# Gate and up weights of a Strassen-style SwiGLU: two transfers of 512 KB a set in place of four of 256 KB, and operand buffers with the contraction step outside

## The reference

```python
def encoder_layer(x, ...):
    xn = rms_norm(x, norm1)
    proj = xn @ w_in
    ...                               # Hyena long convolution and windowed attention
    mixed = jnp.concatenate([rms_norm(y_hy, hy_gain), rms_norm(y_at, at_gain)], axis=-1)
    h = x + mixed @ w_out
    gu = rms_norm(h, norm2) @ w_gate_up          # (rows, 1024) @ (1024, 5632)
    gate, up = jnp.split(gu, 2, axis=-1)
    return h + (jax.nn.silu(gate) * up) @ w_down # (rows, 2816) @ (2816, 1024)
```

## Time and profile before

| | |
|---|---|
| median of 3 runs | 3033.96 us (3030.08 to 3036.27) |
| profiled execution, its own time | 3034.69 us |
| profiled execution, span of its instructions | 3032.9 us |
| mean granted TensorE clock | 0.966 of 2.4 GHz |
| TensorE busy with matmuls | 2808.7 us, 93% |
| VectorE, ScalarE, GpSimd busy | 1922.9, 1216.9, 1030.5 us |
| DMA packets in all | 362367, of them under 2 KB 301374 |
| weight transfers of gate and up | 132 and 132, of 256 KB |

### The profile page before, as it was taken

The page is one execution under the profiler, slowest core; times in us unless marked ns, Lnnn a source line. Parts: engine busy times, 40 slices in busy tenths (PEclk is TensorE's granted clock), DMA queues, the critical chain, the costliest instruction groups (busy, mean ns, idle before and its releaser), DMA issues. The chain is left out here.

```text
span 3032.9 us, 38468 instructions
## 1 busy us (share of the span) xinstructions
PE 2808.7 (93%) x14512; PEld 2546.7 (84%) x14512; DVE 1922.9 (63%) x2615; ACT 1216.9 (40%) x1939; POOL 1030.5 (34%) x797
## 2 busy tenths in 40 slices
PE   5988999899897899997799999889999988999998
PEld 4777898788786788885799999879999987999998
DVE  6765676678565666665565665756566575656655
ACT  4443554444444766664322322322232232223221
POOL 4412111122210344345533433443343344334332
PEclk9998999999998999998899999999999999999999
DMA  5475976766695435334322222332222233222221
GB/s 158 136 225 155 262 216 212 239 195 189 188 255 149 117 112 139 110 101 139 104 73 70 67 73 70 108 125 74 69 67 73 70 112 121 78 69 63 77 70 63
DMA packets 362367, 378.56 MB, mean 125 GB/s; under 512 B 43966, under 2 KB 301374, under 8 KB 361895
## 3 DMA queue, kind: packets, MB, share of 16 engines
q1 hardware_dynamic: 330312, 295.75, 33.8%
q0 software_dynamic: 31872, 80.36, 8.1%
HBM read 281.13 MB, written 94.91 MB: 124 GB/s over the span
## 5 line engine op out<-in xcount | busy, mean ns | idle before, releaser
L2502 POOL TENSOR_TENSOR ff_alo_raw<-ff_alo_raw,ff_silu 128x384 f32<-128x384 f32 x132 | 197.1, 1493 | 741.4 <-DVE ff_alo_raw L2703 658.0
L2725 DVE TENSOR_TENSOR ff_h<-ff_h,ff_down 128x512 f32<-128x512 f32 x396 | 265.4, 685 | 157.7 <-PE ff_down L87 157.5
L85 PE MATMUL ff_banks<-ff_xhi,ff_ghi 128*128 128x384 f32 x924 | 317.5, 344 | 34.1 <-DVE ff_glo L2713 23.5
L85 PE MATMUL ff_down<-ff_dhi,ff_ahi 128*128 128x512 f32 x792 | 312.2, 394 | 24.4 <-DVE ff_dlo L2717 16.9
L87 PE MATMUL ff_banks<-ff_xhi,ff_glo 128*128 128x384 f32 x924 | 315.3, 341 | 0.0
L86 PE MATMUL ff_banks<-ff_xlo,ff_ghi 128*128 128x384 f32 x924 | 314.3, 340 | 0.0
L85 PE MATMUL pr_acc<-pr_xhi,pr_whi 128*128 128x386 f32 (+1 forms) x864 | 306.2, 354 | 7.4 <-DVE pr_xlo L1396 7.4
L85 PE MATMUL ff_banks<-ff_xhi,ff_uhi 128*128 128x384 f32 x924 | 310.6, 336 | 2.6 <-DVE ff_ulo L2713 2.6
L86 PE MATMUL ff_down<-ff_dlo,ff_ahi 128*128 128x512 f32 x792 | 311.8, 394 | 0.0
L87 PE MATMUL ff_down<-ff_dhi,ff_alo 128*128 128x512 f32 x792 | 311.6, 393 | 0.0
L86 PE MATMUL ff_banks<-ff_xlo,ff_uhi 128*128 128x384 f32 x924 | 311.0, 337 | 0.0
(11 more groups left out here) (294 smaller groups left out, 6656.5 us busy)
## 6 DMA issues: line engine op xcount, KB each, us to landing
ff_glo_raw<-w_gate_up SPq DMA_DIRECT2D x132, 256.0 KB, 2.9
ff_ulo_raw<-w_gate_up SPq DMA_DIRECT2D x132, 256.0 KB
ff_dlo_raw<-w_down SPq DMA_DIRECT2D x66, 512.0 KB, 4.5
pr_raw<-w_in SPq DMA_DIRECT2D x108, 256.0 KB, 5.6
pr_xs<-x SPq DMA_DIRECT2D x36, 512.0 KB, 4.5
f_dram<-fi_out POOLq DMA_DIRECT2D x32, 512.0 KB, 4.1
fs_a<-f_dram SPq DMA_DIRECT2D x32, 512.0 KB, 6.7
am_q<-q_dram SPq DMA_DIRECT2D x36, 256.0 KB, 4.4
```

Source lines behind the costliest of these rows:

```text
L85: pe.matmul(out, still[0], moving[0], start=start, stop=False)
L2502: pool.tensor_tensor(block(prod, c), block(prod, c), silu[c][:], ALU.mult).then_inc(tempered, 1)
L2725: dve.tensor_tensor(h[j][:, o], h[j][:, o], down(v), ALU.add).then_inc(added, 1)
```

## The change

The dimensions of the weight buffers change places: from 7 blocks x 4 contraction steps x 128 columns to 4 contraction steps x 7 blocks x 128 columns. The blocks are renumbered so that the two column halves of one contraction half are neighbours: A12 and A22 are blocks 0 and 1, A11 and the fourth block are 2 and 3. A transfer then brings both columns' blocks of one contraction half: 128 partitions x 4 steps x 256 columns, runs of 1 KB in memory where they were 512 B. The first of the two waits for step 4 of the set before last, the second for step 5; before, the four waited for steps 0, 3, 4 and 5. In the load ahead of the stage, A12 came after two transfers of rows and now comes with the other weights. Sums, casts and subtractions read and write four runs a partition instead of one. The two parts of the split are now blocks 0 and 1 (1024 elements) and blocks 2 to 6 (2560 elements), and as A11 is in the second, TensorE waits for both parts ahead of step 0.

```diff
-    A11, A12, A22, S3, S1, S2, S4 = range(7)
+    A12, A22, A11, S3, S1, S2, S4 = range(7)
...
-    whi = [at("ghi", [P, 7, 4, P], 186560, F32R), at("uhi", [P, 7, 4, P], SB0, F32R)]
-    wlo, wraw = zip(pair("glo", [P, 7, 4, P], 186560 + 14336), pair("ulo", [P, 7, 4, P], SB0 + 14336))
+    whi = [at("ghi", [P, 4, 7, P], 186560, F32R), at("uhi", [P, 4, 7, P], SB0, F32R)]
+    wlo, wraw = zip(pair("glo", [P, 4, 7, P], 186560 + 14336), pair("ulo", [P, 4, 7, P], SB0 + 14336))
...
-        def bring_w(s, w):
+        def bring_w(s, half):
             q, p = s // 2, s % 2
             c = q % NC
             if s >= 2:
-                sp.wait_ge(multiplied, step_done(s - 2, W_STEP[w]))
+                sp.wait_ge(multiplied, step_done(s - 2, W_STEP[(S3, A22)[half]]))
             else:
                 at_least(sp, mixed, 4 * NTT * p)
-            i, half = {A11: (0, 0), A12: (0, 1), S3: (1, 0), A22: (1, 1)}[w]
-            col = FF * p + (2 * c + i) * P
-            sp.dma_start(wraw[p][:, w], w_gate_up[:, 4 * half:4 * half + 4, col:col + P]).then_inc(w_in[p], 16)
+            col = FF * p + 2 * c * P
+            sp.dma_start(wraw[p][:, :, 2 - 2 * half:4 - 2 * half].rearrange("p k i c -> p k (i c)"),
+                         w_gate_up[:, 4 * half:4 * half + 4, col:col + 2 * P]).then_inc(w_in[p], 16)
...
         def ahead():
             sp.wait_ge(handed_on, 1)
             sp.wait_ge(weighted, all_weighted)
-            for w in (A11, S3, A22):
-                bring_w(0, w)
+            for half in range(2):
+                bring_w(0, half)
             for x in (B11, T3):
                 bring_x(0, x)
-            bring_w(0, A12)
             for x in (B22, B21):
                 bring_x(0, x)
...
-                    for w in (A11, A12, S3, A22):
-                        bring_w(2 * q + 2, w)
+                    for half in range(2):
+                        bring_w(2 * q + 2, half)
...
-                for w, x in ((A11, B11), (A12, B21), (S3, T3), (A22, None)):
-                    if turning and x is not None:
-                        bring_x(g + 1, x)
-                    if q + 1 < NQ:
-                        bring_w(2 * q + 3, w)
+                if turning:
+                    bring_x(g + 1, B11)
+                    bring_x(g + 1, B21)
+                if q + 1 < NQ:
+                    bring_w(2 * q + 3, 0)
+                if turning:
+                    bring_x(g + 1, T3)
+                if q + 1 < NQ:
+                    bring_w(2 * q + 3, 1)
...
-            pool.wait_ge(w_in[p], 64 * (q + 1))
+            pool.wait_ge(w_in[p], 32 * (q + 1))
...
-            pool.tensor_tensor(raw[:, S1], raw[:, S3], raw[:, A22], ALU.add).then_inc(w_summed, 1)
+            pool.tensor_tensor(raw[:, :, S1], raw[:, :, S3], raw[:, :, A22], ALU.add).then_inc(w_summed, 1)
...
                 if at == 0:
-                    pe.wait_ge(w_low, 2 * s + 1)
-                if at == 1:
                     pe.wait_ge(w_low, 2 * s + 2)
...
-                    last = triple(pe, bank(b), (whi[p][:, w, k, :], wlo[p][:, w, k, :]), (xhi[x][:, k, :], xlo[x][:, k, :]), k == 0, k == 3)
+                    last = triple(pe, bank(b), (whi[p][:, k, w, :], wlo[p][:, k, w, :]), (xhi[x][:, k, :], xlo[x][:, k, :]), k == 0, k == 3)
...
-                act.copy(whi[p][:, 0:3], wraw[p][:, 0:3]).then_inc(w_high, 1)
+                act.copy(whi[p][:, :, 0:2], wraw[p][:, :, 0:2]).then_inc(w_high, 1)
             else:
                 act.wait_ge(w_summed, 4 * s + 4)
-                act.copy(whi[p][:, 3:7], wraw[p][:, 3:7]).then_inc(w_high, 1)
+                act.copy(whi[p][:, :, 2:7], wraw[p][:, :, 2:7]).then_inc(w_high, 1)
...
-            p, o = s % 2, slice(0, 3) if part == 0 else slice(3, 7)
+            p, o = s % 2, slice(0, 2) if part == 0 else slice(2, 7)
             dve.wait_ge(w_high, 2 * s + 1 + part)
             dve.wait_ge(w_summed, 4 * s + 4)
-            dve.tensor_tensor(wlo[p][:, o], wraw[p][:, o], whi[p][:, o].bitcast(F32), ALU.subtract).then_inc(w_low, 1)
+            dve.tensor_tensor(wlo[p][:, :, o], wraw[p][:, :, o], whi[p][:, :, o].bitcast(F32), ALU.subtract).then_inc(w_low, 1)
```

More of the change, by code:

```diff
@@ L2425, in main @@
         def main(close):
-            for w in (A11, S3, A22, A12):
-                bring_w(1, w)
+            for half in range(2):
+                bring_w(1, half)
             close()
@@ L2471, in sums @@
             raw = wraw[p]
-            pool.wait_ge(w_in[p], 64 * (q + 1))
+            pool.wait_ge(w_in[p], 32 * (q + 1))
             if s >= 2:
                 pool.wait_ge(multiplied, step_done(s - 2, 6))
-            pool.tensor_tensor(raw[:, S1], raw[:, S3], raw[:, A22], ALU.add).then_inc(w_summed, 1)
+            pool.tensor_tensor(raw[:, :, S1], raw[:, :, S3], raw[:, :, A22], ALU.add).then_inc(w_summed, 1)
             pool.wait_ge(w_summed, 4 * s + 1)
-            pool.tensor_tensor(raw[:, S2], raw[:, S1], raw[:, A11], ALU.subtract).then_inc(w_summed, 1)
+            pool.tensor_tensor(raw[:, :, S2], raw[:, :, S1], raw[:, :, A11], ALU.subtract).then_inc(w_summed, 1)
             pool.wait_ge(w_summed, 4 * s + 2)
-            pool.tensor_tensor(raw[:, S3], raw[:, A11], raw[:, S3], ALU.subtract).then_inc(w_summed, 1)
+            pool.tensor_tensor(raw[:, :, S3], raw[:, :, A11], raw[:, :, S3], ALU.subtract).then_inc(w_summed, 1)
             pool.wait_ge(w_summed, 4 * s + 3)
-            pool.tensor_tensor(raw[:, S4], raw[:, A12], raw[:, S2], ALU.subtract).then_inc(w_summed, 1)
+            pool.tensor_tensor(raw[:, :, S4], raw[:, :, A12], raw[:, :, S2], ALU.subtract).then_inc(w_summed, 1)
             pool.wait_ge(w_summed, 4 * s + 4)
@@ L2607, in weight_high @@
             if part == 0:
-                act.wait_ge(w_in[p], 64 * (q + 1))
+                act.wait_ge(w_in[p], 32 * (q + 1))
                 if s >= 2:
                     act.wait_ge(multiplied, step_done(s - 2, 5))
-                act.copy(whi[p][:, 0:3], wraw[p][:, 0:3]).then_inc(w_high, 1)
+                act.copy(whi[p][:, :, 0:2], wraw[p][:, :, 0:2]).then_inc(w_high, 1)
             else:
                 act.wait_ge(w_summed, 4 * s + 4)
-                act.copy(whi[p][:, 3:7], wraw[p][:, 3:7]).then_inc(w_high, 1)
+                act.copy(whi[p][:, :, 2:7], wraw[p][:, :, 2:7]).then_inc(w_high, 1)
         def down_high(q, i):
```

## The result

| | before | after |
|---|---|---|
| median | 3033.59 us (4 runs, 3030.08 to 3036.27) | 3052.18 us (4 runs, 3046.37 to 3055.0) |
| profiled execution, its span | 3034.69, 3032.9 us | 3046.37, 3044.6 us |
| mean granted clock | 0.966 | 0.967 |

After/before is 1.0059, with an interval of 1.0041 to 1.0078: about 18 us slower. I had forecast +7.8, and up to 3051. The profiled execution of after is its fastest run, so the spans differ by only 11.7.

The account below looks back on a forecast made before the run. TensorE was taken to bound the kernel, busy throughout steady iterations, so only its few existing waits could move: -4.4 at the start and +12.2 at the merged waits gave +7.8, 3041.8 us against the median (+0.26%), range 3033.5 to 3051.

Parts of the forecast that it names:

- 4, "At nothing": Steady iterations: fewer SyncE issues, later block requests and the new wait at steady up sets cost nothing, with 2 us of cover.
- 1 us for 1 us in 30 iterations: Steady up sets: if the 2 us of cover were gone, 30 iterations would pay 1 us each for 1 us.
- Step 3: Iteration 0 and two turns: step 0 waits for the larger part, slow clock after; 4.5, 3.1 and 4.6, together +12.2 us.
- the 2.34 for the last turn: Clock loss after the single wait at the last turn, taken as 2.34 us more because the loss there was 0 before.
- Step 1: Start of the stage: the weight set lands sooner, so GpSimd's sums and `am_xs` come sooner; -4.4 us, bounds -3 and -7.5.
- Step 2: Strided operands: four runs cost VectorE, ScalarE and GpSimd nothing; for GpSimd at most 0.5 us for three more runs.
- the start gave no 7.5: Rival: the start gains its bound of -7.5, so +4.7 in all, 3038.7 us; chance 0.13.
- the clock did not stay up: Rival: TensorE keeps full clock after the single wait, so +0.8 in all, 3034.8 us, not slower; chance 0.12.
- GpSimd paid nothing for runs: Rival: GpSimd pays 0.5 us for each sum, at the start, iteration 0 and turns; +8 on top, 3049.8 us; chance 0.12.
- the transfers did gain: Rival claimed transfers gain nothing, 512 B runs being as fast as 1 KB: +9.5 in all, 3043.5 us; chance 0.08.
- The rule weighed: Skill's 512 B minimum for line rate: longer runs would gain nothing, sum +9.5 instead of +7.8; the forecast went against it.

Follow-up runs that it names:

- e5: The changed kernel with VectorE's second part of the next gate set made one place earlier in steady iterations: 3037.41 us, ratio 1.0018 to the kernel before.
- e2: The kernel before with one edit, TensorE waits for both parts ahead of step 0: 3051.05 us, ratio 1.0057.
- e3: The kernel before with parts of 2 and 5 blocks and one wait for both, old transfers and flat layout: 3055.96 us, ratio 1.0077.
- e1: The changed kernel with the old split (three and four blocks) and the old two waits: 3028.61 us, ratio 0.9979 to the kernel before.
- e4: The kernel before with the fourth weight transfer, A12, ahead of the row transfers at the start: 3029.65 us, ratio 0.9983.
- e6: e1 with four transfers of 256 KB and runs of 512 B again, new layout kept: 3030.75 us, ratio 0.9993 to the kernel before.
- e7: e1 with both parts of the next gate set made ahead of product and down rests in each group's first chunk: 3004.22 us, ratio 0.991 to before.
- e8: The changed kernel with the moves of both e5 and e7: 3014.51 us, ratio 0.9941 to the kernel before.
- e9: e7 with second gate part and down-weight rests made earlier on VectorE in each group's last chunk: 3004.36 us, ratio 0.9896 to the kernel before.
- e10: e4 with e7's VectorE order, so old transfers, flat layout and old split: 3010.84 us, ratio 0.992 to the kernel before.

## Why the prediction was wrong

**The step that failed is 4, "At nothing".** It costed the steady iterations at nothing, after the opening had said of TensorE's existing waits that "the change can only move the time at these places". For the new wait it looked at the up sets alone: 2 us of cover, which is right. The gate sets have none. In the trace of before their second part ended 0.17 us after TensorE had begun step 0, and my own sentence there, 1 us for 1 us in 30 iterations, was the price. It came to 0.42 us in each of 27, 11.4 us in all, where 0 stood. e5 takes these gaps out of the change (about 12 us, with the `ff_dlo` wait) and e2 puts them into the kernel before (9.3 us). All of the earlier trace rows was true as well, and proved nothing: a TensorE that is busy for 100 us tells that no wait ends late, not how close one is.

**Step 3, the mechanism right and the term too large:** 9.0 us for 12.2. The merged waits came, 10.16, 10.37 and 11.32 us long, where "10 to 12" stood, and the clock behind them was 0.62, 0.63 and 0.66 (forecast 0.61). Most of the difference is the position: I let step 0 start where step 1 had, plus 0.2 at the turns, 1.4 + 0.3 in iteration 0. Counted from TensorE's restart before each (on `ff_dlo`, on `ff_ulo`), the single wait ended 1.0 (turn 1), 0.7 (turn 2) and 1.0 us (iteration 0) **sooner** than the wait of step 1 had. At the turns part of that is the `ff_dlo` restart itself, 0.6 and 0.3 later. Against the forecast positions that is 2.8 us less, and the clock's 0.62 to 0.66 makes 0.5 more. For the wait by itself the position was right: in e2, which changes nothing else, the single wait ended 27.8, 68.1 and 67.9 us after those restarts, where the wait of step 1 had ended after 27.9, 67.9 and 68.0. In e3, with the new split but the old transfers, it is 27.2, 68.0 and 67.9, so the earlier ends at the turns seem to have come with the transfers or the layout; one execution of each doesn't settle it. One term rested on luck: the 2.34 for the last turn took the clock of 1.00 there for a property of the place. In e1, e4 and e6, with the same two waits, it was 0.51, 0.72 and 0.72 there, and 1.00 at turn 1 of e4. The up restart of iteration 0 waited 2.2 us longer (2.65 to 4.85) where 2.29 was forecast.

**Step 1, right in its cause, closer in its number than it deserved:** −4.7 for −4.4. The sums could start 4.83 sooner, and the set landed when forecast (8.61 us after the first issue; 1408.1 is 8.8). No sum ran beside a row sum (1.26 us for the first, not 2.00), so `am_xs` began 5.57 sooner, where 4.6 stood; but it took 5.28 us, not 4.41, and the two errors nearly cancel. e4 shows the cause: the place of one transfer alone gives 5.0 us between the medians.

**Step 2, right:** neither VectorE (2820 ns for 2560 elements) nor GpSimd (1290 where it took 1291) pays for four runs.

**The sum:** −4.7 + 9.0 = +4.3 without the steady gaps, which e5 measured as +4.2; with 11.4 for the gaps and about 1.5 for the first `ff_dlo` wait and the end, +17.2. Of the rivals none came: the start gave no 7.5, the clock did not stay up, GpSimd paid nothing for runs, and the transfers did gain, 0.6 us at the start (e6). The rule weighed, that 512 B is enough for line rate (the Trainium skill, DMA: Bandwidth & Descriptors, Specifications), doesn't hold here: 347 and 380 GB/s for 1 KB where 512 B gave 292 and 325 (e1 and e6), and 420 for 4 KB. It decided 1.7 us of the sum and so nothing of the result.

## What to carry to other kernels

When an edit makes a consumer wait for a later part of its operand, look at every kind of place where that wait stands, and compare in the old trace when the part was done with when the consumer began: a part that is done 0.2 us late is invisible while it is not waited for, and costs each time once it is. Count the waits after a change, not only their sum (6 to 29 here), and compare distances between starts too, as short gaps can have no entry (e2: 27 gaps, and only the long waits listed). If a producer waits for one thing with ready work behind it, its list can be reordered: that was worth 0.7% here (e7 against e1), more than any load.

## What I had not expected of the hardware

An operand that came 0.3 us late cost 0.42, since the next matmul was also 0.28 instead of 0.17 behind. `am_xs`, the same instruction of GpSimd, took 4.41 us before and 5.28 after, where VectorE does its row sums at another time. Its length goes with the kernel: 4.41 in before and e2, 3.88 in e3, 5.28 in after, e5 and e8, and 5.81 in e1, e4, e6, e7, e9 and e10. So it follows the order of the loads and the split, which decide what VectorE does beside it; that the one slows the other wasn't tested. The granted clock is another thing of the execution and not of the kernel alone: after the second of two waits it was 0.51, 0.72, 0.74, 0.75 or 1.00 over 6 us.
